# Two decoder blocks on one core: dummy matmuls ahead of the first weights, output stored tile by tile, additions ahead of remainders

## The reference

```python
for l in range(DEPTH):
    h = rms_norm(x, mix_norm_g[l])
    proj = jnp.einsum("bsd,dc->bsc", h, w_in[l])
    ...
    heads = rms_norm(jnp.stack([o_moba, o_mla, o_sb], axis=2), head_out_g[l])
    mixed = jnp.concatenate([heads.reshape(bsz, seq, 3 * GROUP_WIDTH), o_ssm], axis=-1)
    x = x + jnp.einsum("bsc,cd->bsd", mixed, w_out[l])
    h = rms_norm(x, ffn_norm_g[l])
    u = causal_dwconv(jnp.einsum("bsd,df->bsf", h, ffn_w_in[l]), ffn_conv_w[l]) + ffn_conv_b[l]
    gate, up = _split(u, (D_FF, D_FF))
    x = x + jnp.einsum("bsf,fd->bsd", jax.nn.silu(gate) * up, ffn_w_out[l])
```

## Time and profile before

| | before |
|---|---|
| median of three executions | 1905.96 us |
| profiled execution, and its span | 1905.76 us, 1904.0 us |
| TensorE busy | 1859.7 us, 98% of the span |
| VectorE busy | 1102.8 us, 58% |
| ScalarE busy | 725.5 us, 38% |
| transfers | 284.21 MB, 149 GB/s on average |
| mean granted TensorE clock | 0.996 |
| the chain that ended last | TensorE 86%, VectorE 7%, ScalarE 4%, transfers 1% |

### The profile page before, as it was taken

One profiled execution on the slowest core, in us unless ns is written; L12 is line 12 of the kernel. 1 busy time (PEld: TensorE's weight loads), 2 busy tenths in 40 slices (PEclk: granted clock), 3 DMA queues, 4 the chain that ended last, 5 costly groups with the idle time before them and its releaser, 6 DMA issues.

```text
span 1904.0 us, 30993 instructions
## 1 busy us (share of the span) xinstructions
PE 1859.7 (98%) x12696; PEld 1682.7 (88%) x12696; DVE 1102.8 (58%) x1752; ACT 725.5 (38%) x928; POOL 0.2 (0%) x4
## 2 busy tenths in 40 slices
PE   7999999999999999999999999999999999999998
PEld 5788999968889999999858558999999999789998
DVE  4555887544588856765334322566556664536763
ACT  3345554224455544333113222433343332324432
POOL 0000000000000000000000000000000000000000
PEclk9999999999999999999999999999999999999999
DMA  6322455424135544455322332355545453234553
GB/s 222 109 112 72 178 192 205 158 98 156 51 134 176 201 176 168 172 184 182 132 90 100 113 120 77 133 176 185 179 154 177 176 185 135 87 140 157 195 198 113
DMA packets 35746, 284.21 MB, mean 149 GB/s; under 512 B 4688, under 2 KB 6864, under 8 KB 8144
## 3 DMA queue, kind: packets, MB, share of 16 engines
q1 hardware_dynamic: 35664, 283.05, 41.5%
HBM read 281.98 MB, written 1.05 MB: 149 GB/s over the span
## 4 chain that ended last, share of the span: by engine, by line
PE 86%; DVE 7%; ACT 4%; issue 1%; DMA 1%; ACTq 0%; DVEq 0%
PE PS L1188 18%; PE PS L1189 18%; PE PS L1190 18%; PE PS L638 10%; DVE split L1752 3%; PE PS L647 3%; PE PS L615 3%; PE PS L1091 2%; ACT split L1299 2%; PE PS L746 2%; PE PS L718 1%; PE PS L1132 1%; PE PS L661 1%; PE PS L681 1%; PE PS L919 1%
## 5 line engine op out<-in xcount | busy, mean ns | idle before, releaser
L1188 PE MATMUL PS<-Hhi,split 128*128 128x256 f32 (+1 forms) x2080 | 591.8, 285 | 7.5 <-DVE split L1752 7.4
L1752 DVE TENSOR_TENSOR split<-wa,split 128x2048 fp32r<-128x2048 f32 (+1 forms) x174 | 436.9, 2511 | 272.6 <-ACT split L1299 272.6
L1189 PE MATMUL PS<-Hlo,split 128*128 128x256 f32 (+1 forms) x2080 | 591.1, 284 | 0.0
L1190 PE MATMUL PS<-Hhi,split 128*128 128x256 f32 (+1 forms) x2080 | 589.3, 283 | 0.0
L1299 ACT CAST split<-wa 128x2048 fp32r<-128x2048 f32 (+1 forms) x174 | 362.0, 2080 | 145.2 <-PE PS L1190 145.2
L1188 PEld LDWEIGHTS PS<-Hhi,split 128*128 128x128 f32 x2080 | 391.7, 188 | 12.4 <-DVE split L1752 9.0
L1190 PEld LDWEIGHTS PS<-Hhi,split 128*128 128x128 f32 x2080 | 390.8, 188 | 0.0
L1189 PEld LDWEIGHTS PS<-Hlo,split 128*128 128x128 f32 x2080 | 390.6, 188 | 0.2
L1188 PE MATMUL PS<-hidhi,split 128*128 128x256 f32 (+1 forms) x1088 | 310.2, 285 | 6.4 <-DVE hidlo L2329 3.5
L1190 PE MATMUL PS<-hidhi,split 128*128 128x256 f32 (+1 forms) x1088 | 308.9, 284 | 0.0
L1189 PE MATMUL PS<-hidlo,split 128*128 128x256 f32 (+1 forms) x1088 | 308.1, 283 | 0.0
(11 more groups left out here) (281 smaller groups left out, 1693.9 us busy)
## 6 DMA issues: line engine op xcount, KB each, us to landing
wa<-in_wfi SPq DMA_DIRECT2D x126, 1024.0 KB, 4.8
wa<-in_wfo SPq DMA_DIRECT2D x48, 1408.0 KB, 6.1
wa<-in_wmix SPq DMA_DIRECT2D x26, 2048.0 KB, 8.0
wa<-in_wmix SPq DMA_DIRECT2D x4, 1536.0 KB, 6.3
H<-in_wfi SPq DMA_DIRECT2D x3, 1024.0 KB, 10.1
G<-in_wfi SPq DMA_DIRECT2D x3, 1024.0 KB, 4.8
wa<-in_wmix SPq DMA_DIRECT2D x2, 1024.0 KB, 4.7
wa<-in_wmix SPq DMA_DIRECT2D x2, 768.0 KB, 9.3
```

The lines of the kernel that those rows point to most:

```text
L1188: pe.matmul(o, hi, xhi, start=first, stop=False)
L1189: pe.matmul(o, hi, xlo, start=False, stop=False)
L1190: return pe.matmul(o, lo, xhi, start=False, stop=last)
L1752: dve.tensor_tensor(out=wlo[n % 2][:, 0:width], in0=wa[:, c % 2, 0:width], in1=whi[n % 2][:, 0:width].bitcast(F32), op=ALU.subtract).then_ ...
```

## The change

Four edits are made together.

1. SyncE issues the positions behind the first weights. VectorE makes all eight tiles of G ahead of the eight additions of squares.
2. TensorE runs 18 matmuls of 128x128 by 128x256 in float32 on the cleared tile of W0 into PSUM, ahead of its first wait for weights. They start once W0 is cleared. Nothing reads their result.
3. In both early mixers `project_out_ahead` makes all eight additions and then the eight remainders. ScalarE makes the eight squares and then the eight roundings. The first early chunk is rounded ahead of the roots of the last head norm, and its remainder formed ahead of that norm's end.
4. The output is stored by eight transfers of 128 KB, each as soon as its tile is added, in place of one.

```diff
-            sp.dma_start(posi, positions.to_broadcast([P, SEQ])).then_inc(S.pos_in, 16)
...
             sp.dma_start(wa[:, 0, MIX1[0] // 2:MIX1[0]], first[:, MIX1[0] // 2:MIX1[0]]).then_inc(WA[0], 16)
+            sp.dma_start(posi, positions.to_broadcast([P, SEQ])).then_inc(S.pos_in, 16)
...
-            sp.wait_ge(S.x_tile, KD * 5 * DEPTH)
-            sp.dma_start(out, X[:, :, META:TT]).then_inc(S.out_written, 16)
-            sp.wait_ge(S.out_written, 16)
+            for m in range(KD):
+                sp.wait_ge(S.x_tile, KD * (5 * DEPTH - 1) + m + 1)
+                sp.dma_start(out[:, m, :], X[:, m, META:TT]).then_inc(S.out_written, 16)
+            sp.wait_ge(S.out_written, 16 * KD)
...
                 if l == 0:
                     take()
+                    pe.wait_ge(S.act_done, 4)
+                    for _ in range(18):
+                        pe.matmul(PS[:, 0, 0:SEQ], W0[:, 3, 0:P], W0[:, 3, 0:SEQ], start=True, stop=True)
                     pe.wait_ge(S.w_first, 16)
...
                 squares_of(head_norm(l, 0))
-                roots_of(head_norm(l, 0))
                 act.wait_ge(S.ss_done, upto(S.ss_done))
                 round_early(0)
+                roots_of(head_norm(l, 0))
                 round_early(1)
                 take(KD // PER1)
                 for m in range(KD):
                     act.wait_ge(S.x_tile, upto(S.x_tile))
                     act.activation(square_place(m), X[:, m, META:TT], ACT.Square).then_inc(S.sq_apart, 1)
+                for m in range(KD):
                     round_tile(SEQ, META, m, f"ffng{l}", hidhi, AHEAD)
...
-                for j in range(KD // 2):
-                    dve.wait_ge(S.prod_done, before + j + 1)
-                    for m in (2 * j, 2 * j + 1):
-                        add_tile(m, SEQ, META, 1.0, out_place(m))
-                    for m in (2 * j, 2 * j + 1):
-                        rest_of_tile(m, SEQ, META, gain, hidhi, hidlo, AHEAD)
+                for m in range(KD):
+                    dve.wait_ge(S.prod_done, before + m // 2 + 1)
+                    add_tile(m, SEQ, META, 1.0, out_place(m))
+                for m in range(KD):
+                    rest_of_tile(m, SEQ, META, gain, hidhi, hidlo, AHEAD)
...
                 normalised(ssm_out(l)).then_inc(S.ss_done, 1)
+                rest_early(0)
                 normalised(head_norm(l, 0)).then_inc(S.mb_done, 1)
-                rest_early(0)
                 dve.wait_ge(S.mb_done, upto(S.mb_done, 2))
                 rest_early(1)
...
             for m in range(KD):
                 hp_tile(m, SEQ, META, "mixg0")
+            for m in range(KD):
                 add_square(SEQ)
```

## The result

The changed kernel took 1893.37 us in the median of five runs (1892.06 to 1895.20), the kernel before 1904.25 us beside it; the ratio is 0.994, with an interval of 0.9929 to 0.9950. By the bound of 2% that is no change.

What follows compares the result with a forecast made beforehand. TensorE, busy for 98% of the span, was taken to bind the kernel; start 1.2, mixers 5.0 and store 2.5 sum to 8.7 us off the profiled 1905.76, giving 1897.1 us, range 1894.0 to 1901.5.

Steps and rivals of the forecast that it cites:

- nearly all of the time is a stream of matmuls that this change leaves alone: Whole span: TensorE is busy for 98%, so gains lie only where its stream has not started, runs slowly, waits or is over.
- The start: Start of the kernel: TensorE wins 2.4 us but VectorE's H binds, leaving 1.2 us, between a 1.1 loss and 1.8 gain.
- the zeros would not warm the engine: Rival at the start: dummies on zeros stay slow and end at 17.5 us; 1900.8 us in all, chance 0.13.
- the two signs that it named for being wrong: Feed-forward's first streamed chunk not released earlier along with the root, or positions landing behind 13.2 us at the start.
- TensorE keeps all: Rival: TensorE keeps its 2.4 us at the start, or the feed-forward takes the whole 3.1; 1894.7 us, chance 0.12.
- The mixers: Ends of the two early mixers: the root comes 2.5 us earlier in each, 5.0 us in all (3.6 to 6.2).
- the longer wait for the first streamed chunk: Feed-forward behind an early mixer: TensorE starts 3.1 us earlier, the chunk only 2.5, so the wait grows by 0.6 us.
- the gain was not given back: Rival: the chunks' own chain binds the feed-forward's first pairs, so the mixers' gain is lost; 1902.1 us, chance 0.10.
- The store: End of the kernel: the last transfer carries an eighth, landing about 2.2 us after issue, not 4.7; 2.5 us gained.
- Slower than before: Rival in the early mixers: VectorE's first remainder delays the head norm, 5 us late in each; 1907 us, chance 0.02.

Runs made afterwards that it cites:

- each half of the start alone: Kernel before with only the positions' transfer and VectorE's additions reordered, or with only the dummy matmuls; single times 1903.40 and 1902.20 us, beside 1902.26 of before.
- the order: Kernel before with only VectorE's eight tiles of G ahead of the additions and positions issued behind the first weights, no dummies; 1903.40 us, executed once.
- the clearing: Changed kernel with VectorE's clearing of VP moved ahead of its wait for the input; 1891.50 us, ratio 0.9934 to the kernel before.

## Why the forecast was wrong

Its median is 1897.1 - 1893.4 = 3.7 us too high.

- **The base, 1.5 us.** The forecast was taken off one profiled execution of 1905.76 us, and I compared that only with a median of three. The runs beside the changed kernel gave 1904.25. The kernel before scatters with the low stretches: over 53 runs its mean is 1908.0 us at a mean granted clock of 0.994, 1905.3 at 0.996 and 1902.9 at 0.998, about 1.3 us for each 0.001. The profiled execution, at 0.996 and with two full stretches of 6.8 us, is on the slow side of it.
- **The sum, 2.2 us** (10.9 measured by medians, 8.7 forecast), and this is the step that failed: "nearly all of the time is a stream of matmuls that this change leaves alone". I took that stream as running at one pace, looked at the clock only in the first 20 us, and had no term for the two places at which it falls to 1.2 GHz. The range had none either; a scatter of single runs was left outside it. In the two profiled executions these places make 1.9 + 2.2 us of the 13.6. By medians their share is smaller, and it can be narrowed. Single runs of the two kernels at the same mean granted clock stand 9.3 us apart at 0.998 (1902.9 in 11 runs, 1893.6 in 9) and 9.4 at 0.997 (1904.05 in 8, 1894.6 in 3). That is the forecast's 8.7 and the 0.7 us of the feed-forward between 530 and 729 us, which the forecast had as untouched too. The rest of the 10.7 to 11.2 us by medians goes with the clock: 0.998 in the mean of 15 runs of the changed kernel, 0.996 in 63 of before. Not all of that difference is worth time, as in the trace of before 2.4 us at the lower level stand behind the last matmul (0.8 us at the rate above), so 1 us or so, by my estimate, is what the rarer low stretches gave. One place where the change makes them rarer is the mixers' end, shown above. That it does so at the even and the odd mixer is not shown.

Point by point:

- *The start, 1.2 us forecast, 1.25 in the trace.* The mechanism held: 1.84 us of wait for VectorE, ended by H. VectorE's G and additions took 12.85 - 6.90 = 5.95 us (5.8 to 6.4 forecast), and the positions cost no wait. The dummies ended at 11.6, not 12.6 (11.5 to 13.2 over 13 traces): they start ten us before the real work did, and the pace rises by its own moment, not after a fixed number of matmuls. As forecast, this changed nothing. That the zeros would not warm the engine is out: 36 records in 9.53 us are x at 0.427 and the rest at 0.216, which gives x = 8. The part alone gave 2.9 us by its median; the 0.7 us of these that lie between 530 and 729 us had no place in the forecast. Nor had it seen that the first group of before waited for the seventh tile of G (11.79 + 0.35 us) and not for weights, which were there at 11.0. The positions landed at 12.35, so neither of the two signs that it named for being wrong came; it was wrong in the sum.
- *TensorE keeps all.* Out: each half of the start alone ended at the same wait for VectorE. The time that this rival named, 1894.7, was nearer than mine, for another reason.
- *The mixers, 5.0 us forecast, 4.9 in the traces, 5.5 by the median of the part alone.* The mechanism held. The root at 4.5 us behind the last product, no gap in the sums, and the longer wait for the first streamed chunk (184.53, wait 1.24 us, against 0.41 in the earlier trace rows: 0.8 more, 0.6 forecast) all came as told. From the root to that chunk it takes 11.65 us, before 11.68: the gain was not given back.
- *The store, 2.5 us forecast, 2.8 in the trace.* By the median of the part alone it is 1.8, with an interval of 0.6 to 4.0. The last store lands in 1.9 us, not 2.2: what I took as a fixed part of 1.83 us is smaller for the small store, too. Stores in the middle take up to 6.6 us to land and nobody waits for them, as the trace's distance of 7.8 us had said.
- *Slower than before* never came near: VectorE's first remainder ended at 159.1, ahead of the head norm at 159.59.

## What to carry to other kernels

When a kernel's gain is a fraction of a per cent, read the granted clock over the whole span before setting up the sum: 3.4 or 6.8 us at the lower level cost 1.3 or 2.2 us here, as much as an edit was worth, and it makes one profiled execution a poor base. Ask of two edits at one place what each gives alone: at the start and at the mixers' end one would have given almost all. And when two edits come together, look which wait ended last before: the first group's start moved by 3.3 us with the order, and it was VectorE's tile that had held it, not the weights. After an edit look at which engine binds now, since its work may move into idle time of its own, as the clearing did: 0.6 to 1.2 us more at the start in the traces, 1.9 by the median.

## What the runs showed of the hardware that I had not expected

- TensorE falls to 1.2 GHz in the middle of a stream at 98% busy. A stretch began within or at most 1.4 us behind a run of 4.2 us or more of matmuls with 8 columns in all 17 traces that have it in one piece, though the engine shows no gap, and behind idle times of 3.6 us in 12 of 15 traces at the odd mixer. The changed kernel's own three traces had 0, 0 and 6.8 us at the odd mixer and 3.4, 6.8 and 3.4 at the even one.
- The end of a mixer as before, with gaps of 1.00 us in the sums of squares, brings a stretch of 3.4 us in four of six traces, the new end in none of 14. The Trainium skill (TensorE: Matmul & The Clock Gate, HAM oscillation) tells of idle waits that bring the lower level back; the odd mixer's traces agree, at 1.3 or 2.2 us a time.
- At the start the granted clock reads 1.00 while the first matmuls run at half pace; in the middle of the program it reads 0.50 when they do. The trace's own list of clock changes begins at 17.4 us in before and at 5.1 in after, where the pace rises, so 1.00 ahead of that is no reading.
- Matmuls on zeros raise the pace as others do: 28 of 36 records ran at the full one in after.
- A transfer of 128 KB in small packets, issued ahead, held back the first weights by 1.8 us.
